# One product of 128 rows for a gated head's scores, in place of one of 64 and one of 40

## The reference, cut to what matters

```python
log_f = jax.nn.log_sigmoid(f_in + b_f)            # (256, 8)
cum_f = jnp.cumsum(log_f, axis=1)
# per block of 128 queries, per head of 64
lb = jnp.einsum('bthd,bshd->bhts', qb, k_b)       # qb is scaled by 1/8
lb = lb + fq[..., None] - cum_f_keys[:, :, None, :]
lb = jnp.where(causal[None, None], lb, -jnp.inf)
pb = jax.nn.softmax(lb, axis=-1)
ob = jnp.einsum('bhts,bshd->bthd', pb, v_b)
```

## Time and profile before

| | |
|---|---|
| median of 3 runs (range) | 1466.08 us (1460.47 to 1467.77) |
| the profiled execution | 1466.05 us, span 1464.8 us |
| mean granted TensorE clock | 0.984 |
| PE busy | 1420.0 us, 97% |
| DVE busy | 941.9 us, 64% |
| ACT busy | 722.8 us, 49% |
| POOL busy | 228.6 us, 16% |

### The profile page before, as it was taken

The page is one execution under the profiler, slowest core; times in us unless marked ns, Lnnn a source line. Parts: engine busy times, 40 slices in busy tenths (PEclk is TensorE's granted clock), DMA queues, the critical chain, the costliest instruction groups (busy, mean ns, idle before and its releaser), DMA issues.

```text
span 1464.8 us, 23172 instructions
## 1 busy us (share of the span) xinstructions
PE 1420.0 (97%) x9623; PEld 1265.3 (86%) x9623; DVE 941.9 (64%) x1506; ACT 722.8 (49%) x1054; POOL 228.6 (16%) x190
## 2 busy tenths in 40 slices
PE   7899999999999999998999999999999999899998
PEld 5887799999898899996777899999789988799997
DVE  4764486676785866677556166656556989565555
ACT  3534344545343454543555354444456775454453
POOL 2571200000000000002722500000124233100000
PEclk9998999999999999999999999999999999899999
DMA  8432145655463455552512345655354434345551
GB/s 299 148 130 115 54 170 181 229 188 187 170 221 148 159 201 202 194 180 90 198 58 87 116 183 191 208 195 177 113 199 158 155 121 180 138 173 195 197 198 58
DMA packets 36554, 240.40 MB, mean 164 GB/s; under 512 B 3873, under 2 KB 6241, under 8 KB 8930
## 3 DMA queue, kind: packets, MB, share of 16 engines
q1 hardware_dynamic: 36450, 238.92, 45.2%
HBM read 236.27 MB, written 2.64 MB: 163 GB/s over the span
## 4 chain that ended last, share of the span: by engine, by line
PE 86%; DVE 6%; ACT 3%; issue 2%; POOL 2%; DMA 1%; SPq 0%; ACTq 0%; DVEq 0%
PE ps L363 25%; PE ps L326 15%; PE ps L327 15%; PE ps L328 15%; PE ps L485 2%; PE ps L492 2%; POOL wlo L276 1%; DVE ar L2112 1%; ACT whi L268 1%; PE ps L816 1%; PE ps L1621 1%; PE ps L984 1%; PE ps L473 1%; PE ps L1886 1%; PE ps L714 1%
## 5 line engine op out<-in xcount | busy, mean ns | idle before, releaser
L326 PE MATMUL ps<-XS,whi 128*128 128x256 f32 x2088 | 600.8, 288 | 15.1 <-POOL wlo L276 5.4
L327 PE MATMUL ps<-XS,whi 128*128 128x256 f32 x2088 | 596.3, 286 | 0.0
L328 PE MATMUL ps<-XS,wlo 128*128 128x256 f32 x2088 | 596.0, 285 | 0.0
L283 DVE TENSOR_TENSOR wlo<-raw,whi 128x2048 fp32r<-128x2048 f32 x163 | 372.4, 2287 | 120.8 <-ACT whi L268 120.7
L268 ACT ACTIVATE whi<-raw 128x2048 fp32r<-128x2048 f32 x204 | 388.7, 1907 | 120.3 <-PE ps L363 83.2
L326 PEld LDWEIGHTS ps<-XS,whi 128*128 128x128 f32 x2088 | 406.5, 195 | 21.2 <-issue 9.2
L327 PEld LDWEIGHTS ps<-XS,whi 128*128 128x128 f32 x2088 | 406.5, 195 | 1.8 <-issue 0.2
L328 PEld LDWEIGHTS ps<-XS,wlo 128*128 128x128 f32 x2088 | 406.2, 195 | 0.0
L363 PE MATMUL ps<-whi,MS 128*128 128x512 f32 x1024 | 290.7, 391 | 0.0
L276 POOL TENSOR_TENSOR wlo<-raw,whi 128x512 fp32r<-128x512 f32 x162 | 211.7, 1341 | 493.6 <-ACT whi L268 410.0
L363 PEld LDWEIGHTS ps<-whi,MS 128*128 128x128 f32 x1024 | 189.6, 188 | 37.9 <-issue 0.4
(11 more groups left out here) (282 smaller groups left out, 1363.2 us busy)
## 6 DMA issues: line engine op xcount, KB each, us to landing
raw<-in_up SPq DMA_DIRECT2D x88, 1024.0 KB, 4.8
raw<-in_down SPq DMA_DIRECT2D x44, 1024.0 KB, 4.8
raw<-in_hg_t SPq DMA_DIRECT2D x16, 1024.0 KB, 4.8
raw<-in_od_t SPq DMA_DIRECT2D x8, 1024.0 KB, 5.1
raw<-in_ev_a SPq DMA_DIRECT2D x7, 1024.0 KB, 8.1
raw<-in_wa_o SPq DMA_DIRECT2D x6, 1024.0 KB, 4.7
raw<-in_hg_o SPq DMA_DIRECT2D x6, 1024.0 KB, 4.7
raw<-in_ev_o SPq DMA_DIRECT2D x4, 1024.0 KB, 7.0
```

Source lines behind the costliest of these rows:

```text
L283: ve.tensor_tensor(lo[:, 0:w], r[:, 0:w], hi[:, 0:w].bitcast(F32), ALU.subtract).then_inc(w_lo_v)
L326: pe.matmul(d, hi[:, c], S[:, k, 0:256], start=(k == 0), stop=False)
L327: pe.matmul(d, hi[:, c], S[:, k, 256:512], start=False, stop=False)
L328: last = pe.matmul(d, lo[:, c], S[:, k, 0:256], start=False, stop=(k == 7))
```

## The change

The two heads that shared 128 partitions get 256 columns each, over all 128 partitions. `QX` and `KX` are 2048 columns wide, with four pairs of heads; the even head of a pair has its 64 rows of queries or keys in partitions 0 to 63, the odd one in 64 to 127. The free half of a head's columns holds the rows that stood in `L` and `rv`: sums of the logarithms and ones in `QX`, ones in the head's own row and negated sums in `KX`, and zeros elsewhere. The score is then one fp32 product over 128 rows and the mask. `QX` takes the place of `QB` and `KB`, `KX` that of `rv`.

- ACT: each of the eight copies of queries or keys becomes two, over 64 partitions each (`heads_of`). The wait for the transfer `d_skw` moves ahead of the first.
- DVE, early: the three memsets of `L` are gone, and the one of `gb` (128 x 2048) becomes two of 64 x 1024.
- DVE, after the scan: a wait for `d_skw`, two memsets of 64 x 1024 in `QX`, one negation of 104 x 256, and then for each half a copy, a memset, a copy and a product of 8 x 1024, where there were a copy 8 x 256, a copy 8 x 2048, a negation 8 x 256 and a product 8 x 2048.
- PE: the products of L985 are gone, and those of L984 use 128 rows; the wait for `e_cum` goes from 6 to 8.

```diff
-        L = R(256)
+        R(256)
-        QI, KI, QB, KB, VB = R(1024), R(256), R(1024), R(1024), R(1024)
+        QI, KI, QX, VB = R(1024), R(256), R(2048), R(1024)
-        RH = gb2
-        rv = RH.rearrange("p (h t) -> p h t", h=8)
+        KX = gb2
+        hx4 = lambda ap, r: ap.rearrange("p (c r t) -> p c r t", r=2, t=256)[:, :, r, :]
...
-            pe.wait_ge(e_cum.sem, 6)
+            pe.wait_ge(e_cum.sem, 8)
...
-                pe.matmul(o[:, a:b], QB[q, c + 128 * tt:c + 128 * tt + 128], KB[q, c:c + b - a], start=True, stop=False)
-                pe.matmul(o[:, a:b], L[g, 128 * tt:128 * tt + 128], rv[g, h, 0:b - a], start=False, stop=False)
+                pe.matmul(o[:, a:b], QX[:, c + 128 * tt:c + 128 * tt + 128], KX[:, c:c + b - a], start=True, stop=False)
                 last = pe.matmul(o[:, b - 128:b], identb, cmb, start=False, stop=True)
...
+            def heads_of(m, i, dst, c, scale=1.0):
+                ac.wait_ge(w_done, DONE[m])
+                b = bank[4 + [0, 1, 2, 0, 1, 2, 3, 0, 0, 0, 3, 3][m - ea]]
+                for r in range(2):
+                    p = slice(64 * r, 64 * r + 64)
+                    ins = ac.activation(dst[p, 512 * c + 256 * r:512 * c + 256 * r + 256], b[p, 256 * i:256 * i + 256], ACT.Copy,
+                                        scale=scale)
+                ins.then_inc(e_ac.up())
...
-                out_of(ea + 4 + j, 0, KB[:, 256 * j:256 * j + 256])
-                out_of(ea + 4 + j, 1, QB[:, 256 * j + 256:256 * j + 512], 0.125)
+                heads_of(ea + 4 + j, 0, KX, j)
+                heads_of(ea + 4 + j, 1, QX, j + 1, 0.125)
...
-            ve.memset(L, 0.0).then_inc(dv.up())
-            ve.wait_ge(dv.sem, dv.n)
-            ve.memset(L[32:40, :], 1.0)
-            ve.memset(L[96:104, :], 1.0)
             ve.wait_ge(m_tp.sem, 4)
-            ve.memset(RH, 0.0).then_inc(dv.up())
+            for r in range(2):
+                ve.memset(hx4(KX, r)[64 - 64 * r:128 - 64 * r], 0.0).then_inc(dv.up())
...
-            for a in (0, 64):
+            ve.wait_ge(d_skw, 16)
+            for r in range(2):
+                ve.memset(hx4(QX, r)[64 - 64 * r:128 - 64 * r], 0.0).then_inc(dv.up())
+            ve.tensor_scalar(FZ[z, :], FW[z, :], -1.0, None, ALU.mult).then_inc(dv.up())
+            ve.wait_ge(dv.sem, dv.n)
+            for r in range(2):
+                a = 64 - 64 * r
                 b = a + 32
-                ve.tensor_copy(L[a:a + 8, :], FW[a:a + 8, :]).then_inc(e_cum.up())
-                ve.tensor_copy(rv[a:a + 8], ident[a:a + 8, a:a + 8].unsqueeze(2).to_broadcast([8, 8, 256])).then_inc(e_cum.up())
-                ve.tensor_scalar(FZ[b:b + 8, :], FW[b:b + 8, :], -1.0, None, ALU.mult).then_inc(dv.up())
-                ve.wait_ge(dv.sem, dv.n)
-                ve.tensor_tensor(rv[b:b + 8], ident[b:b + 8, b:b + 8].unsqueeze(2).to_broadcast([8, 8, 256]),
-                                 FZ[b:b + 8, :].unsqueeze(1).to_broadcast([8, 8, 256]), ALU.mult).then_inc(e_cum.up())
+                own = lambda p: ident[p:p + 8, p:p + 8].rearrange("p (c r) -> p c r", r=2)[:, :, r:r + 1].to_broadcast([8, 4, 256])
+                row = lambda ap: ap.unsqueeze(1).to_broadcast([8, 4, 256])
+                ve.tensor_copy(hx4(QX, r)[a:a + 8], row(FW[a:a + 8, :])).then_inc(e_cum.up())
+                ve.memset(hx4(QX, r)[b:b + 8], 1.0).then_inc(e_cum.up())
+                ve.tensor_copy(hx4(KX, r)[a:a + 8], own(a)).then_inc(e_cum.up())
+                ve.tensor_tensor(hx4(KX, r)[b:b + 8], own(b), row(FZ[b:b + 8, :]), ALU.mult).then_inc(e_cum.up())
             select(16)
```

More of the change, by code:

```diff
@@ L977, in score_b @@
         def score_b(o, h):
-            q = slice(64 * (h % 2), 64 * (h % 2) + 64)
-            g = slice(64 * (h % 2), 64 * (h % 2) + 40)
-            c = 256 * (h // 2)
+            c = 256 * h
             pe.wait_ge(e_ac.sem, max(AT_QB[h // 2], AT_KB[h // 2]))
@@ L1083, in even_act @@
             out_of(ea + 3, 0, CT)
-            out_of(ea + 3, 1, QB[:, 0:256], 0.125)
             ac.wait_ge(d_skw, 16)
+            heads_of(ea + 3, 1, QX, 0, 0.125)
             for j in range(3):
                 act_weights(ea + 6 + j)
-                out_of(ea + 4 + j, 0, KB[:, 256 * j:256 * j + 256])
-                out_of(ea + 4 + j, 1, QB[:, 256 * j + 256:256 * j + 512], 0.125)
+                heads_of(ea + 4 + j, 0, KX, j)
+                heads_of(ea + 4 + j, 1, QX, j + 1, 0.125)
             act_weights(ev_ + 3)
@@ L1094, in even_act @@
             act_weights(eb + 2)
-            out_of(eb, 0, KB[:, 768:1024])
+            heads_of(eb, 0, KX, 3)
             out_of(eb, 1, QA[:, 0:256])
```

## The result

The changed kernel took 1450.67 us, the median of 5 runs (1448.27 to 1453.85). The kernel before, timed beside it, took 1463.07 us, also the median of 5 (1460.47 to 1467.77). The ratio is 0.9906, with a 95% interval of 0.9886 to 0.9925. The profiled execution took 1453.85 us with a span of 1452.5, so it is 12.2 us shorter than the profiled one before (1466.05). It was the slowest of its five: three of them took 1448.27 to 1450.67 us at a mean granted clock of 0.989 to 0.991, and two, the profiled one among them, 1452.92 and 1453.85 us at 0.985 to 0.986.

A forecast was written before the change was run, and what follows sets the result against it. TensorE, with 86% of the chain of waits, was taken as the bound, soft at 62 to 66 and 105 to 121 us. Terms 2.5 + 3.6 + 6.3 = 12.4 us off 1466.05 gave 1453.7; own range 1451 to 1456, 8 in 10: 1450 to 1459.

The forecast's parts named there:

- part 1: DVE chain behind the scan: shorter VectorE instructions hold GpSimd up less, project of ea+6 starts earlier; 2.5 us net.
- head 0: First gated head, between other TensorE work: 1.29 us instead of 2.01, so 0.72 less.
- heads 1 to 3: Back-to-back heads to the end of L971: 7.7 us instead of 14.02; gain 6.3, about 2.2 products and 4 clock.
- heads 4 to 7: Heads between other TensorE work: 0.72 us less each, TensorE's step 2.43 us instead of 3.15.
- the second wait that I had priced: TensorE idle 1.8 us before project of ea+6, for GpSimd's eighth instruction; a lowered clock after it would cost 1.7.
- Part 2: ScalarE's eight copies out of PSUM become two each: 0.33 us more each, bounds nothing and 0.38, all hidden.
- Part 3: TensorE's scores: a gated head costs 1.29 us instead of 2.01; five heads among other work save 3.6.
- the 2.7 that the prediction named as a sign of being wrong: Forecast is wrong if TensorE's step for heads 4 to 7 stays above 2.7 us.
- Rival C: Loop of heads 4 to 7 becomes bound by ScalarE and VectorE, 2.9 us turn into waits; 1456.5 us; chance 0.07.
- Rival A: Clock still falls in heads 1 to 3: gain there 2.9 us instead of 6.3; 1457.0 us; chance 0.20.
- B: 3-D broadcast copies run at half rate, GpSimd's eight instructions end at 73.9 as before; 1456.2 us; chance 0.09.
- D: VectorE's 104x256 tensor_scalar isn't let in during GpSimd's run, TensorE waits; 2.1 us slower, 1468.2 us; chance 0.05.

The follow-up runs named there:

- ScalarE's rows: Changed kernel, but ScalarE copies the scan's result into both tensors and the one-hot blocks are built before the scan; two jobs: 1449.29 us (0.9892), 1449.95 us (0.9899).
- the holds doubled: Changed kernel with each copy and tensor_tensor of 8x1024 behind the scan issued twice; 1456.17 us, ratio 0.9941.

## Why the time was predicted 3 us too high while the sum held

The gain was right: 12.4 us forecast, 12.2 from profiled to profiled execution, and 12.4, 11.2 and 12.9 between the medians of three jobs. The time was not: 1450.67 us measured, 1453.7 forecast. The four pieces, forecast and measured: part 1, 2.5 and 2.18; head 0, 0.72 and 1.21; heads 1 to 3, 6.3 and 7.03; heads 4 to 7, 2.88 and 3.09. They add up to 13.5, and 1.3 was taken back behind the stage, where I had put nothing ("Nothing behind the stage idles long enough to take it back"). Two errors of about one microsecond cancelled, so that the sum meets the measured gain to the tenth is luck; that it lies within 1.5 us of it in every pairing above is not.

**The level.** The step that failed is the one from the gain to the time: "The median of the runs shown, 1466.08, is the same as that execution". It took one profiled execution, and a median of three, for the kernel's level, and that was 3.0 us too high. With two more executions the median of before was 1463.07, and over eleven it was 1464.21 and 1465.47, in a spread of 8 us (1460.24 to 1468.34). The gain subtracted from 1463.07 gives 1450.7, which is what was measured; from 1466.05 it gave 1453.7. The measured median lies within the range for 8 in 10 and 0.3 us below the forecast's own.

What the runs show in its place is that one execution does not stand for the median. For the two of the kernel after at a clock of 0.985 to 0.986, as in the profile before (0.984), the forecast is exact to a microsecond (1452.92 and 1453.85); the median of the five fell among the three at 0.989 to 0.991. In the two later jobs the same kernel had medians of 1453.02 (four executions, all at 0.985 to 0.986) and 1452.59 (three of six at 0.989 to 0.991), 0.7 and 1.1 us below the forecast. In the two profiles that show it, the difference lies behind head 8 (1334.3 and 1329.6 us, above), where the change has no code; why an execution takes one or the other is open.

**Part 1** went turn by turn as worked out. The fourth GpSimd instruction was to end at 63.6 and ended at 64.1; the eighth at 71.1 and ended at 71.0. Reckoned from GpSimd's first instruction the piece is 2.3 to 2.4 us, with 2.5 forecast. The memset of 1024 was put at 0.91 and took 0.91. Two sizes were off. VectorE pauses 0.27 us ahead of each memset here, which shifted the first turns by half a microsecond and let the chain end at 73.8 instead of 72.3. And ea+5's products took 7.5 us again, at a lowered clock, though the idle time ahead was 2.15 instead of 4.31; by the time they were done at 71.7 GpSimd was ready, so the second wait that I had priced (1.8 us) wasn't there. In the third profile of the kernel after the clock held there, and the wait came (72.81 us, 0.95 idle). The two events replace each other, which is why the piece is nearly the same: I had named the fall for the second idle time, and it came after the first.

The prediction cited the Trainium skill (SBUF — State Buffer, section Who interferes with whom): a memset does not contend with GpSimd, copies in a two-port mode and instructions with two SBUF inputs do. The trace agrees: GpSimd's 1.29 us beside two memsets, 1.79 beside a copy, 2.26 beside a tensor_tensor.

**Part 2** cost nothing, as said. Two copies over 64 partitions take 0.77 us, where two over 128 took 0.66. I read that as 0.33 for one, and it isn't: each lasts 0.38 in both kernels, but the second one over 128 started 0.29 after the first, and over 64 it starts 0.39 after it, just above the upper bound that I gave.

**Part 3** was mis-sized in the cost of a head. I took 0.49 for a pair of 256 columns from a latent head, which was right, but kept 0.16 for the mask, the price that it has behind few-row products. Behind 128 rows it is 0.05 to 0.06, and the pair of 128 columns is 0.22 behind `project` and 0.42 behind the value product, whose output has 64 partitions. The experiments show why the mask and the pair behind `project` are cheap: what is paid is the change between products over part of the rows and over all. The 0.42 is another matter, since the value product runs over all 128 rows; no run here isolates it. Head 0, which stands between `project`s, saved 1.21, 0.49 more than its term. The mask product of the latent head stood in the trace of before with 0.06 (at 132.41), and I didn't use it. Behind the cross products head 4 saved 1.19 (2.03 to 0.84), heads 5 to 7 saved 1.01 each (2.03 to 1.02): 4.22, while the piece is 3.09. TensorE's timeline shows where 0.63 of the rest went; first the kernel before, then after:

```profile
127.91 0.48 PE L1015 MATMUL ps<-ar 64*128 64x256 f32 x1
127.92 0.48 PE L984 MATMUL ps<-ar 64*128 64x128 f32 x2
```

```profile
114.78 0.70 PE L1014 MATMUL ps<-ar 64*128 64x256 f32 x2
115.41 0.49 PE L984 MATMUL ps<-gb,ar 128*128 128x128 f32 x2
```

Before, the latent query's product over 64 rows and head 7's score product over the other 64 rows ran at the same time; the padded product needs all 128, so the latent query's 0.63 us stand alone. That is a price of the padding that I had not put in. The other 0.50 are a wait of TensorE for L857 behind head 5, ahead of the transposes at 111.37 (0.28), and the 0.22 by which these take longer behind a wait (0.55 for three instead of 0.33). VectorE and GpSimd of the kernel after show what L857 waited for:

```profile
109.94 1.37 DVE L857 TENSOR_SCALAR ar<-ar 128x256 f32<-128x256 f32 x1
```

```profile
107.43 5.00 POOL L276 TENSOR_TENSOR wlo<-raw,whi 128x512 fp32r<-128x512 f32 x4 [4.83 <-ACT whi L268]
```

The third of these four GpSimd instructions runs from 109.89 to 111.15, and L857, a moment later, ends only at 111.31: it is one more turn of GpSimd's. Two of the steps between heads 4 and 8 are 2.77 us (112.71 to 115.48 to 118.25), above the 2.7 that the prediction named as a sign of being wrong. The latent query's 0.63 is in both, which the sign hadn't reckoned with; without it they are 2.14, against the 2.43 of the forecast. Rival C is that half microsecond and no more.

TensorE's page of the Trainium skill (TensorE: Matmul & The Clock Gate, section LDWEIGHTS) says that a weight load over 32 rows takes as long as one over 128. By that alone a pair of 64 rows and one of 128 would cost the same; the runs have 0.41 and 0.22, and 0.63 and 0.49, and what a chain row holds is a product together with its load. No run here times a load by itself.

**Heads 1 to 3.** Rival A occurred in none of six profiles with the single product over 128 rows (three of after, two with ScalarE's rows, one with the holds doubled), and not with twice or four times the products. But the argument was only half right. "Rows over the whole array" stands as far as it was tested, since no stretch of 128-row products lost the clock, although few rows alone don't bring the fall (four 64-row products, twice); "half the length" does not, since length made no difference. And L714's 32 rows do not by themselves bring the fall at 28 to 30 us that I had put down to them: L714 runs in the kernel after just the same, 2.84 us from 26.84, and the window 28 to 33 above has 1.00. In each of the fourteen profiles the clock fell either between 16 and 24 us or between 28 and 33, never in both; the second profile of the kernel before has the first of the two. Of the 7.03 us some 4.5 are the clock and 2.5 the products less the wait, with 4 and 2.2 forecast (an estimate: 2.42 between the end of head 3's scores and head 4, and 8.18 for the three heads less 3 x 2.02). The new wait ahead of head 3 was 0.79 us instead of 0.35, on head 1's exponentials; the cheaper heads reach it sooner. It is paid out of their saving.

**Rivals B and D.** B is refuted by the copies' hold of 0.48 to 0.53, half of the 0.99 beside a copy of twice the elements (2.25 less 1.26, at 65.81 in the kernel before): the middle dimension costs nothing. D did not occur: no instruction of the chain waited longer than one turn of GpSimd's. The wait of 11.49 us itself was that execution's and not the kernel's. In the second profile of the kernel before the same instruction, again in the middle of GpSimd's run, is:

```profile
87.14 1.46 DVE L1187 TENSOR_SCALAR ar<-ar 128x384 f32<-128x384 f32 x1
```

In the profile after (L1199 there) it takes 1.49 us at 87.44. What made VectorE wait through nine turns that one time is open.

## What to carry to other kernels

Don't count a small product by its rows or columns alone: look at what stands ahead of it. A product over part of the rows between products over all of them costs 0.14 to 0.19 us on its way in and 0.10 on the way out, so padding it to 128 rows is worth more than its own time says; against that stands the neighbour on the other rows beside which it ran for nothing. When VectorE and GpSimd share a stretch on whose end TensorE waits, count GpSimd's turns one by one, and give the copies to ScalarE where it has room: that was worth 3.7 and 2.6 us by the medians, 0.9 and 2.4 in the traces. And take the starting level from more runs than three, and the gain from the profile, piece by piece and each from its own start: the same program spread over 8 us.

## What the runs showed of the hardware that was not expected

- The granted clock held at 1.00 through about 10 us of 64-row products with a mask product behind every four, in two executions, and fell to 0.50 within the shorter stretch with one or two, in four.
- After TensorE had idled for about 2 us ahead of tile ea+5, the clock fell in its products in six of twelve profiles (idle 1.86 to 2.15 us) and held in the other six (1.90 to 2.59). After the 4.3 us of the kernel before it fell both times.
- VectorE stands still for 0.27 us ahead of five of the six memsets of 1024 elements in the kernel after; the sixth, at 40.32, comes out of a longer wait. The two memsets of 8x256 in the kernel before (38.47 and 38.83) followed within 0.11 us. What makes the difference wasn't tried.
- A ScalarE copy of 256 columns out of PSUM lasts 0.38 us over 64 partitions and over 128; the next one started 0.39 us behind it over 64, and 0.29 over 128.
- Whole stretches of lowered clock move from one execution of a kernel to the next: in the kernel before from 28 to 33 us to 16 to 24, in the kernel after from 64 to 68 to 38 to 42. They moved GpSimd's start at ea+5 between 57.35 and 59.97 us.
